# A sequence mixer rebuilt: order of its columns, who computes the convolution's taps, and how its layer norm is computed

## The reference, cut to what matters

```python
def conformer_conv_heads(v, gate, conv_w, conv_b, ln_g, ln_b):
    u = v * jax.nn.sigmoid(gate)
    u = lax.conv_general_dilated(u, conv_w[:, None, :], window_strides=(1,),
        padding=[(15, 15)], feature_group_count=B_WIDTH) + conv_b      # 31 taps, each channel by itself
    u = layernorm(u by heads of 128, ln_g, ln_b)
    return silu(u)
h = rmsnorm(x, g) @ w_in_ab         # 1536 columns: a (512), v (512), gate (512)
y = concat(fnet_heads(a), conformer_conv_heads(v, gate, ...))
x = x + y @ w_out_ab
```

## Time and profile before

| | us |
|---|---|
| median of three runs | 1693.8 (1688.9, 1693.8, 1695.8) |
| profiled execution | 1688.3 |
| its span, first to last instruction | 1686.5 |
| stretch up to the mixer's first product | 1176.3 |
| projection in the mixer | 1176.3 to 1211.85 |
| Fourier part and taps | 1211.85 to 1241.5 |
| output products and layer norm | 1241.5 to 1276.7 |
| first product of the first feed-forward part | 1281.27 |

### The profile page before, as it was taken

The page is one execution under the profiler, slowest core; times in us unless marked ns, Lnnn a source line. Parts: engine busy times, 40 slices in busy tenths (PEclk is TensorE's granted clock), DMA queues, the critical chain, the costliest instruction groups (busy, mean ns, idle before and its releaser), DMA issues.

```text
span 1686.5 us, 21872 instructions
## 1 busy us (share of the span) xinstructions
PE 1557.9 (92%) x8609; PEld 872.5 (52%) x8609; DVE 677.9 (40%) x966; ACT 438.1 (26%) x716; POOL 66.4 (4%) x90
## 2 busy tenths in 40 slices
PE   5999999999998898999988888886999999999998
PEld 3887533333333223333223222223857998789986
DVE  3575632322322222232222212214775665466654
ACT  3565311111111010111111000003525444354443
POOL 4032000000000000000000000000000000400000
PEclk9999999999999999999999999998999999989999
DMA  9748999999999999999999999998335555455540
GB/s 359 205 159 294 396 387 416 415 417 415 416 417 414 417 416 416 417 415 417 416 414 416 411 416 416 410 417 297 132 100 186 178 194 180 150 182 181 189 161 25
DMA packets 152931, 534.50 MB, mean 317 GB/s; under 512 B 9809, under 2 KB 72936, under 8 KB 117824
## 3 DMA queue, kind: packets, MB, share of 16 engines
q1 hardware_dynamic: 150832, 530.18, 80.7%
q0 software_dynamic: 1936, 1.98, 0.5%
HBM read 531.06 MB, written 1.05 MB: 316 GB/s over the span
## 4 chain that ended last, share of the span: by engine, by line
PE 38%; DMA 15%; DVE 3%; ACT 1%; issue 1%; SPq 0%; DVEq 0%
DMA ring<-in_w_mlp 15%; PE ps L474 8%; PE ps L476 8%; PE ps L475 8%; PE ps L852 6%; PE ps L870 2%; PE ps L1199 1%; PE ps L877 1%; PE ps L823 1%; PE ps L1359 0%; DVE arena L2019 0%; PE ps L1256 0%; PE ps L1265 0%; PE ps L1207 0%; DVE arena L2106 0%
## 5 line engine op out<-in xcount | busy, mean ns | idle before, releaser
L852 PE MATMUL ps<-ring,arena 128*64 128x512 f32 x2048 | 493.2, 603 | 21.0 <-DMA ring<-in_w_mlp 20.7
L870 PE MATMUL ps<-ring,arena 128*64 128x512 f32 x1024 | 239.8, 605 | 33.3 <-DMA ring<-in_w_mlp 26.3
L852 PEld LDWEIGHTS ps<-ring,arena 128*64 128x64 f32 x2048 | 128.0, 136 | 266.0 <-issue 193.5
L1392 DVE TENSOR_TENSOR wl<-ring,wh 128x1024 fp32r<-128x1024 f32 x132 | 162.0, 1232 | 136.1 <-ACT wh L2230 136.1
L474 PE MATMUL ps<-hth,wh 128*128 128x256 f32 x704 | 201.1, 286 | 0.6 <-DVE htl L2042 0.5
L475 PE MATMUL ps<-htl,wh 128*128 128x256 f32 x704 | 198.8, 282 | 0.0
L476 PE MATMUL ps<-hth,wl 128*128 128x256 f32 x704 | 198.1, 281 | 0.0
L1853 DVE TENSOR_TENSOR arena<-ps,arena 128x1024 f32<-128x1024 f32 x68 | 83.3, 1225 | 254.1 <-PE ps L877 243.8
L2230 ACT ACTIVATE wh<-ring 128x1024 fp32r<-128x1024 f32 x132 | 139.3, 1060 | 148.7 <-PE ps L476 148.7
L870 PEld LDWEIGHTS ps<-ring,arena 128*64 128x64 f32 x1024 | 70.3, 138 | 197.0 <-issue 125.8
L1873 DVE TENSOR_TENSOR arena<-ps,arena 128x512 f32<-128x512 f32 x34 | 23.5, 692 | 362.0 <-PE ps L870 358.9
(11 more groups left out here) (420 smaller groups left out, 1768.5 us busy)
## 6 DMA issues: line engine op xcount, KB each, us to landing
ring<-in_w_mlp SPq DMA_DIRECT2D x384, 1024.0 KB, 21.5
ring<-in_w_ada SPq DMA_DIRECT2D x24, 1024.0 KB, 14.4
ring<-in_ffn_w_gate SPq DMA_DIRECT2D x22, 1024.0 KB, 5.2
ring<-in_ffn_w_up SPq DMA_DIRECT2D x22, 1024.0 KB, 5.2
ring<-in_ffn_w_down SPq DMA_DIRECT2D x22, 1024.0 KB, 4.8
ring<-in_w_in SPq DMA_DIRECT2D x10, 768.0 KB, 12.7
ring<-in_w_in_ab SPq DMA_DIRECT2D x6, 1024.0 KB, 12.4
ring<-in_w_out SPq DMA_DIRECT2D x4, 1024.0 KB, 8.2
```

What stands on the lines that cost most here:

```text
L852: t = pe.matmul(PS[64 * g:64 * g + 64, HB[hb][ns], :], x[:, k8, :], u[:, f:f + 512], start=False, stop=k8 == 7)
L870: t = pe.matmul(PS[64 * g:64 * g + 64, 3, :], a4[:, kc, 64 * kg:64 * kg + 64], u[:, c, g * 512:(g + 1) * 512], start=k8 == 0, stop=k8 == 7)
L1392: dve.tensor_tensor(l, src, h.bitcast(F32), ALU.subtract).then_inc(*V.tick((st, "lo", n)))
```

## The change

- Columns go by gate pairs: the ring order and the pieces become v0 v1, gate0 gate1, v2 v3, gate2 gate3 (`AB`). The sigmoid and u are made for each half as soon as its gate is there. The Sigmoid table is asked for before the projection's second piece pair.
- TensorE has no taps and ScalarE no diagonals. NPT is 11 now and means taps that ScalarE multiplies (a copy with a weight per partition, `shifted`), into eight buffers of 512 columns, the first into `PC`; GpSimd adds them up in `PC`, one after the other. VectorE does the other 20, accumulating in PSUM (`cp`), and adds both (`cv`). Its low parts, the taps of half 0 and u of half 1 are interleaved by hand; so are ScalarE's high parts and shifts, and its last shifts of half 1 stand between the copies of the Fourier part.
- The layer norm centres by one product with identity minus 1/128 (`CMX`). ScalarE squares straight from PSUM and copies the centred half. The squares are summed with the squares as the stationary operand and one moving column, four products that leave the sums of 512 tokens as [128, 4]; root and reciprocal work on four columns. VectorE makes four diagonal matrices of them, and one product with ones spreads them over the partitions. Half 0's layer norm is done between taps of half 1. Gain and bias go into the sigmoid's scale and bias.
- The output products are put in another order around these, and (1, 1) of blocks 4 and 5 goes ahead of the transposes.

```diff
+AB = (0, 2, 1, 3)
+NPT = 11
...
     post = len(order)
-    order += [("abc", c) for c in range(4)] + [("abr", kk) for kk in range(2)] + [("dft",), ("fm",)]
...
+        at = at_s
+        assert 6144 <= 2 * NFF * 256
...
+        PC = v1(o_ht, 1024).rearrange("p (c n) -> p c n", c=4)
+        DG4 = v1(o_ht + 1024, 512)
+        CMX, RST = v1(o_ht + 1536, 128), [v1(o_ht + 1664 + 4 * h, 4) for h in range(2)]
+        def pair(buf, h):
+            return buf[:, 2 * h:2 * h + 2, :].rearrange("p c n -> p (c n)")
+        def tap_buf(h, w):
+            q = (h * (NPT - 1) + w - 1) % 8
+            return (XN if q < 4 else XS).rearrange("p t n -> p (t n)")[:, 512 * (q % 4):512 * (q % 4) + 512]
+        def cp(c):
+            return PS[:, c // 2, (c % 2) * 256:(c % 2) * 256 + 256]
...
+            def centre(h):
+                pe.wait_ge(*done("centring"))
...
+                pe.wait_ge(*done(("u", 1)))
+                pe.matmul(PS[:, 2 + h, :], CMX, pair(CV, h), start=True, stop=True).then_inc(*P.tick(("ln centred", h)))
+            def spread_sums(h):
...
+                for j in range(4):
+                    t = pe.matmul(PS[:, h, j:j + 1], pair(SGm, h)[:, 128 * j:128 * j + 128], ones[:, 0:1], start=True,
+                                  stop=True)
+                t.then_inc(*P.tick(("ln var", h)))
+            def spread_roots(h):
+                pe.wait_ge(*done(("ln diag", h)))
+                pe.matmul(PS[:, h, :], ones, DG4, start=True, stop=True).then_inc(*P.tick(("ln spread", h)))
+            pe.wait_ge(*done("vectors"))
+            pe.wait_ge(*landed(("dft",)))
+            pe.wait_ge(*done(("a", 1)))
+            over_tokens(0)
+            over_tokens(1)
+            over_width(0)
+            over_tokens(2)
+            over_width(1)
+            pe.wait_ge(*landed(("fm",)))
+            mapped(0)
+            over_tokens(3)
+            mapped(1)
+            centre(0)
+            over_width(2)
+            over_width(3)
+            mapped(2)
+            spread_sums(0)
+            mapped(3)
...
+            part = out_ab(0)
...
+            spread_roots(0)
...
+            centre(1)
...
+            some_out_ab(0, 0, range(4, 6))
+            some_out_ab(0, 1, range(4, 6))
+            spread_sums(1)
+            some_out_ab(1, 0, range(4, 6))
+            spread_roots(1)
...
+            some_out_ab(1, 0, range(6, 8))
+            some_out_ab(1, 1, range(4, 6))
...
+            some_out_ab(1, 1, range(6, 8))
...
+            dve.scalar_tensor_tensor(out=CMX, in0=ones, scalar=-1.0 / 128, in1=ident, op0=ALU.mult, op1=ALU.add).then_inc(
+                *V.tick("centring"))
+            def u_of(h):
+                dve.wait_ge(*done(("g sigmoid", h)))
+                dve.wait_ge(*done("u zeroed"))
+                dve.tensor_tensor(uT[:, 2 * h:2 * h + 2, 15:271], PS[:, h, :].rearrange("p (c n) -> p c n", c=2),
+                                  SGm[:, 2 * h:2 * h + 2, :], ALU.mult).then_inc(*V.tick(("u", h)))
...
+                last = [("u", h), ("u", h)]
...
+                        dve.wait_ge(*done(last[m]))
+                        last[m] = ("tap", h, w, m)
...
+                            dve.tensor_scalar(cp(c), uT[:, c, 0:256], cw2[:, c, 0:1], cb2[:, c:c + 1], ALU.mult,
+                                              ALU.add).then_inc(*V.tick(last[m]))
...
+                            dve.scalar_tensor_tensor(out=cp(c), in0=uT[:, c, w:w + 256], scalar=cw2[:, c, w:w + 1],
+                                                     in1=cp(c), op0=ALU.mult, op1=ALU.add).then_inc(*V.tick(last[m]))
+                    yield
+                dve.wait_ge(*done(("tapped", h, NPT - 1)))
...
+                dve.tensor_tensor(pair(CV, h), PS[:, h, :], pair(PC, h), ALU.add).then_inc(*V.tick(("cv", h)))
...
+            def some(gen, n):
+                for _ in range(n):
+                    next(gen, None)
+            def ln_diag(h):
...
+                dve.reciprocal(RST[h], RST[h]).then_inc(*V.tick())
...
+                dve.tensor_tensor(DG4.rearrange("p (j n) -> p j n", j=4),
+                                  ident.rearrange("p (j n) -> p j n", j=1).to_broadcast([128, 4, 128]),
+                                  RST[h].rearrange("p (j n) -> p j n", n=1).to_broadcast([128, 4, 128]),
+                                  ALU.mult).then_inc(*V.tick(("ln diag", h)))
+            def ln_scaled(h):
+                dve.wait_ge(*done(("ln copied", h)))
+                dve.wait_ge(*done(("ln spread", h)))
+                dve.tensor_tensor(pair(CV, h), pair(CV, h), PS[:, h, :], ALU.mult).then_inc(*V.tick(("ln scaled", h)))
+            def ln_out(h):
...
+                dve.wait_ge(*done(("ln affine", h)))
+                dve.tensor_tensor(YT[:, 4 + 2 * h:6 + 2 * h, :].rearrange("p c n -> p (c n)"), pair(PC, h), pair(SGm, h),
...
+            for n in range(2, 6):
+                lo("ab", n)
+            u_of(0)
+            t0, t1 = taps(0), taps(1)
+            lo("ab", 6)
+            some(t0, 1)
+            for n in range(7, 10):
+                lo("ab", n)
+                some(t0, 2)
+            u_of(1)
+            lo("ab", 10)
+            some(t0, 2)
+            lo("ab", 11)
+            some(t0, 32)
+            some(t1, 10)
+            ln_diag(0)
+            some(t1, 4)
+            ln_scaled(0)
+            some(t1, 4)
+            ln_out(0)
+            some(t1, 32)
...
+            ln_diag(1)
+            ln_scaled(1)
+            dve.wait_ge(*V.now())
+            for c in (2, 3):
+                dve.tensor_scalar(PC[:, c, :], CV[:, c, :], lg2[:, c:c + 1], lb2[:, c:c + 1], ALU.mult,
+                                  ALU.add).then_inc(*V.tick(("ln affine", 1)))
+            ln_out(1)
...
+            def sigmoid_table():
+                act.wait_ge(*S.now())
+                act.activation(rs[:, 4:5], eps, ACT.Sigmoid).then_inc(*S.tick())
+            def g_sigmoid(h):
+                act.wait_ge(*done(("ab", "used", 4 * h + 3)))
+                act.activation(pair(SGm, h), PS[:, 2 + h, :], ACT.Sigmoid).then_inc(*S.tick(("g sigmoid", h)))
+            sigmoid_table()
+            for n in range(2, 6):
+                hi("ab", n)
+            g_sigmoid(0)
+            def shifted(h):
+                act.wait_ge(*done(("u", h)))
+                for w in range(NPT):
+                    at = 31 - NPT + w
+                    q = h * (NPT - 1) + w - 1
+                    if w and q >= 8:
+                        act.wait_ge(*done(("tapped", (q - 8) // (NPT - 1), (q - 8) % (NPT - 1) + 1)))
+                    for m in range(2):
+                        c = 2 * h + m
+                        o = tap_buf(h, w)[:, 256 * m:256 * m + 256] if w else PC[:, c, :]
+                        t = act.activation(o, uT[:, c, at:at + 256], ACT.Copy, scale=cw2[:, c, at:at + 1])
+                    t.then_inc(*S.tick(("shifted", h, w)))
+                    yield
+            def some(gen, n):
+                for _ in range(n):
+                    next(gen, None)
+            part = shifted(0)
+            for n in range(6, 10):
+                hi("ab", n)
+                some(part, 2)
+            g_sigmoid(1)
...
+            some(part, 1)
...
+            some(part, 3)
+            part = shifted(1)
+            some(part, 6)
...
+            def ln_square(h):
+                act.wait_ge(*done(("ln centred", h)))
+                act.activation(pair(SGm, h), PS[:, 2 + h, :], ACT.Square).then_inc(*S.tick(("ln square", h)))
+            def ln_copied(h):
+                act.activation(pair(CV, h), PS[:, 2 + h, :], ACT.Copy).then_inc(*S.tick(("ln copied", h)))
+            def ln_root(h):
+                act.wait_ge(*done(("ln var", h)))
+                act.activation(RST[h], PS[:, h, 0:4], ACT.Sqrt, scale=1.0 / 128, bias=eps5).then_inc(
+                    *S.tick(("ln root", h)))
+            def ln_sigmoid(h):
+                act.wait_ge(*done("vectors"))
+                act.wait_ge(*done(("ln scaled", h)))
+                for c in (2 * h, 2 * h + 1):
+                    act.activation(SGm[:, c, :], CV[:, c, :], ACT.Sigmoid, scale=lg2[:, c:c + 1],
+                                   bias=lb2[:, c:c + 1]).then_inc(*S.tick(("ln sigmoid", h)))
+            some(part, 1)
...
+            some(part, 1)
...
+            some(part, 1)
...
+            some(part, 1)
+            cs(2)
+            some(part, 2)
...
+            cs(3)
...
+            root_table()
+            ln_square(0)
...
+            ln_copied(0)
...
+            ln_root(0)
...
+            sigmoid_table()
+            ln_sigmoid(0)
+            for c in range(2):
+                act.activation(PC[:, c, :], CV[:, c, :], ACT.Identity, scale=lg2[:, c:c + 1],
+                               bias=lb2[:, c:c + 1]).then_inc(*S.tick(("ln affine", 0)))
+            root_table()
...
+            ln_square(1)
+            ln_copied(1)
+            ln_root(1)
+            sigmoid_table()
+            ln_sigmoid(1)
...
```

(13 more changed lines are left out.)

142 lines of the change are left out of this document (12 added, 130 removed).

## The result

The changed kernel takes 1682.3 us, median of 8 runs (1677.74 to 1685.42), beside 1691.12 for the kernel before on the same chip (8 runs, 1688.41 to 1695.8). The ratio is 0.9943, 95% interval 0.9928 to 0.9959: 8.8 us saved. A second measurement of the same kernel, on another occasion, gave 1680.68 against 1691.02, ratio 0.9931 (0.9914 to 0.9948), 10.3 us. By the first interval the saving lies between 6.9 and 12.2 us. The profiled execution took 1680.08 us with a span of 1678.3, 8.2 less than the 1686.5 of before.

A forecast was written before the change was run, and what follows sets the result against it. TensorE and VectorE were near their limit to 1242, the layer norm the limit to 1265.25. 10.55 us, less 0.3, plus 0.5, gave 10.7, say 10.5, off the 1693.8 median: 1683.3 us, range 1677 to 1692.

The forecast's parts named there:

- the walk: Recomputed timeline from projection through layer norm: TensorE's last release at 1254.7 instead of 1265.25, 10.55 us earlier.
- 0.3 for the late piece: Projection: five VectorE low parts lose 0.5 us each to GpSimd's additions, making TensorE 0.3 us late.
- Rival B: Projection: each of five low parts waits 1.3 us for a whole GpSimd addition; saving 6.5, time 1687.3; chance 0.15.
- Taps: VectorE's taps stay at 0.40 us each writing PSUM; ScalarE's shifts 0.40 each; GpSimd's additions 1.5 us.
- Rival E: VectorE's PSUM writes take 0.69 us a tap; 7.5 us slower, 1701; chance 0.03.
- Fourier part: First token product at 1213.1 against 1219.6; output products begin at 1229.4 against 1241.52, 12.1 us earlier.
- rival C: Fourier part: ScalarE's shifts, ahead of its copies, wait for GpSimd to free buffers; saving 5, time 1688.8; chance 0.12.
- Layer norm: TensorE, not VectorE, is last before half 1's centring, after output products to 1244.0; sums with one moving column take 1.0.
- T: TensorE's last release, for half 1's layer-norm result: forecast 1254.7 instead of 1265.25, 10.55 us earlier.
- both big reciprocals: Layer norm: VectorE's two reciprocals over 512 columns, 6.5 us, claimed to be on the path and removed.
- The table load: ScalarE before half 0's square: 1.28 + 0.2 us counted; a skill's 1.38 drain, left out, would make the saving 9.1.
- Rival D: Fourier part onward: thinner TensorE work lowers its clock from 1213 to 1252; 15.5 us slower, 1709; chance 0.05.

The follow-up runs named there:

- after: First trace of the changed kernel: stretch (VectorE's first x2 addition to first feed-forward product) 103.69 us, against 113.72 before.
- narrow_adds: Changed kernel with each of GpSimd's 20 additions adding one column of 512, the rest left out: stretch 103.99 us, against 103.69.
- adds_late: Changed kernel with GpSimd's additions held until VectorE's last low part of the projection is done: stretch 110.18 us, against 103.69.
- new_norm: Kernel before with the new layer norm alone, TensorE keeping its taps: stretch 112.65 us, against 113.72.
- ln_first: Changed kernel with the earlier table load, TensorE's layer-norm steps and half 1's taps put first, one table switch less: 1674.63 us, ratio 0.9903 to the kernel before.
- after_again: Second trace of the unchanged changed kernel, as a control: stretch 103.31 us, against 103.69 in the first.
- table_early: Changed kernel with the root table loaded earlier on ScalarE and half 0 centred one step later on TensorE: stretch 103.59 us, against 103.69.
- sbuf_taps: Changed kernel with VectorE's taps accumulated in SBUF in place of PSUM: stretch 116.99 us, against 103.69.
- plain_order: Changed kernel with the columns in their old order, v0 to v3 then gate0 to gate3: stretch 109.24 us, against 103.69.
- fill_stop: Changed kernel with four output-product records moved ahead of TensorE's wait for half 1's result: stretch 103.50 us, against 103.69.
- early_filled: Changed kernel with both the earlier root-table load and four output-product records moved into TensorE's stop: stretch 101.68 us, against 103.69.
- old_norm: Changed kernel with the old layer norm, its steps set between the taps: stretch 107.41 us, against 103.69.
- before: Trace of the kernel before the change: stretch 113.72 us; median of 8 runs 1691.12 us.

## Why the prediction was right, step by step

The forecast was 1683.3 us and a saving of 10.5; the kernel took 1682.3, with 8.8 and 10.3 us saved in two measurements and 10.03 in the stretch. That the time came out within 1.0 us is in part luck: the base of 1693.8, a median of three runs, was 2.7 above the 1691.12 of eight, and the saving in the medians was 1.7 smaller than forecast, and the two errors offset each other. The saving itself, 10.03 or 10.19 in the traces, rests on the walk, which came true step by step. The times below are those of after less the 1.98 us by which its stretch began later (by the mixer's first product they are 0.16 earlier still).

- **Projection.** u of half 0 came at 1190.8 (forecast 1190.7). The five low parts that meet GpSimd took 9.65 us where 6.15 is undisturbed: 0.7 each, not 0.5. TensorE was last released by one (bracket of 0.63) and lost about 1.0 us, not 0.3: the first token product comes 37.76 us behind the mixer's first product, and 36.73 in narrow_adds. The term "0.3 for the late piece" is the one that was mis-sized. Rival B has its place right, and its price is 1.0 us (narrow_adds), not 4.3.
- **Taps.** 22 in 8.70 us, 0.40 apart; mean 479 ns, against 477 in SBUF before. Only the first tap of each block is longer (0.99 for two, has 0.73). Rival E is out. ScalarE's shifts were 497 ns each in duration but 0.40 apart (16 in 6.49 us), as the sum had it. GpSimd's additions were 1.47 us on average; (1,2) was in time.
- **Fourier part.** First token product 1214.2 (1213.1 + 0.3), first output product 1230.1 (1229.4 + 0.3), the sums with one moving column 0.95 for eight records (1.0). GpSimd held up nobody; rival C needs the late additions of adds_late.
- **Layer norm.** Half 1 centred at 1244.84 (1244.0 + 0.3), T at 1255.6 (1254.7 + 0.3). VectorE waited 2.25 us for the first root (2 said) and nobody felt it. The rest behind T was 15.62 for 16.02; I had said 0.5 less.
- **The path.** The forecast named TensorE's order as what ends last before half 1's centring. Its rows show it (1243.58 ready, 1246.82 begun), and new_norm and ln_first bear it out: with the taps on TensorE the norm's new form gives 1.1, and ln_first takes out another 5.5 with the work nearly the same.
- **What was read wrong.** The prediction called both big reciprocals, 6.5 us, part of the path before. new_norm takes both away and gains 1.1: TensorE had other records to fill most of that time, it stood still for 0.15 and 2.48 us only the earlier trace rows, and the new norm gave it two spreading products of 0.86 us more to do. It did no harm, because the saving was not added up from what was removed but from a new walk to T.
- **The table load.** ScalarE's timeline of after:

```profile
1226.00 0.38 ACT L2685 ACTIVATE arena<-ps 128x256 f32<-128x256 f32 x1
1226.39 1.28 ACT L2590 ACT_TABLE_LOAD   x1
1227.69 0.20 ACT L2590 ACTIVATE arena<-arena 128x1 f32<-128x1 f32 x1
```

The load begins 0.01 us after the copy ahead of it has ended, and the next activation starts 1.30 us after the load began. The drain of about 1.38 that the Trainium skill (ScalarE: Activation LUTs, What ACT_TABLE_LOAD costs) adds isn't in these rows, and leaving it out of the sum was right.

- **Rival D**, the clock, did not come where I had put it: the granted clock was 1.00 from 1178 to 1257.6 in spite of TensorE's pauses. It does live in this stretch, behind the stop at T, and cost 1.5 to 3.0 us in five of the variants. In the changed kernel it cost nothing in the two executions that were traced; of the others no trace tells. That I had no term for that place did no harm by chance more than by reasoning. TensorE's pause before the last transposes became longer (3.78, has 2.72) and these took 2.07 us for 1.41 at a granted clock of 0.50, 1.2 GHz; that is in the 15.62 above. The longer pause need not be the reason: they took 2.07 behind 2.70 us in new_norm and 1.41 behind 2.71 in ln_first.
- **The basis.** Taking the saving off the median and not off the profiled execution (which would have said 1677.8) was nearer to the 1682.3; but the median of three was itself 2.7 too high, as said above.

## What to carry to other kernels

Before costing the operations of a stage, read which engine's own order of instructions releases it: here taking away 6.5 us of reciprocals was worth 1 us while TensorE's own work was the limit, and the changed kernel, with the new norm in it, gave a further 5.5 by other orders alone, an earlier table load among them. If VectorE and GpSimd are to share elementwise work, keep VectorE's accumulator in PSUM (479 ns a tap, against 650 in SBUF beside GpSimd), and expect its remaining instructions on SBUF alone to pay (1.22 became 1.55 on average). And judge small edits on the stretch between two fixed instructions of one trace, and choose the first of them as near to the change as can be: the stretch from the x2 addition repeats within 0.4 us, that from the mixer's first product within 0.03, where the unchanged part ahead varied by 7.

## What was not expected of the hardware

The same stop of TensorE, 2.85 us long, was followed by the full clock in three traces (after, after_again, adds_late: 16 records in 7.10 us) and by a lower one in four (narrow_adds 8.60, table_early and sbuf_taps 8.80, plain_order 10.13), though TensorE's work ahead of it was alike: in all seven the same records stand between the first output product and T, in 25.47 or 25.48 us. With the stop at 1.14 us (fill_stop, early_filled) or gone (ln_first) the clock never fell there. The one stop of 6.09 us (old_norm) was followed by 8.79, and the one of 2.48 (before) by 7.11. What decides between the two outcomes is open; no run here separates it, and it may change from one execution of a kernel to the next.

The clock also explains why savings did not add: from the mixer, table_early alone made the stretch 0.2 us longer and fill_stop changed nothing, and together they gave 1.7.
